# A gather ring of seven slots instead of eight, with one more output-projection slab kept for both tiles of a layer

## What is computed

```
for i in range(2):
    h = h + token_mixer(rms_norm(h), w_in[i], ..., w_o[i])     # proj = h @ w_in; attention; y @ w_o
    h = h + peer_ffn(rms_norm(h), w_query[i], sub_keys[i], u[i], v[i])
    h = h + sigmoid(rms_norm(h) @ w_ple_gate[i]) * (p[i] @ w_ple[i])
# peer_ffn, per token: 8 heads, 16 experts each, out of 128*128
ids, gate = top 16 of (top 16 of s1 + top 16 of s2), per head
pre = u[ids] . x;   out = sum over the 128 pairs of gate * gelu(pre) * v[ids]
```

## Time and profile before

| | us |
|---|---|
| median of three runs | 1560.29 |
| their range | 1559.32 to 1563.16 |
| the profiled execution, its own time | 1557.42 |
| its span, first to last instruction | 1555.6 |
| busy: PE / DVE / ACT / POOL | 1132.1 / 1069.5 / 567.9 / 575.4 |
| first gather issued at | 119.7 |
| last gather issued at | 1513.0 |

### The profile page before, as it was taken

How to read it: one execution, slowest core, us unless ns; L and a number is a source line. 1 busy time by engine, 2 the same in 40 slices (tenths; PEclk the granted TensorE clock), 3 DMA queues, 4 the chain that set the end, 5 groups by cost and what they waited for, 6 DMA issues and landing times.

```text
span 1555.6 us, 18293 instructions
## 1 busy us (share of the span) xinstructions
PE 1132.1 (73%) x6360; PEld 443.9 (29%) x6360; DVE 1069.5 (69%) x2719; ACT 567.9 (37%) x1788; POOL 575.4 (37%) x516
## 2 busy tenths in 40 slices
PE   9996676885658865778566887598555876676666
PEld 6771133351113422325111353245101311111112
DVE  3468986679987345567999536757799765454555
ACT  0503456333333235423333415733233443333332
POOL 0004444445443333435453323434444353333330
PEclk9996878997779978789668998989577976667668
DMA  9148999999999999999999999999999999999992
GB/s 358 65 173 362 416 421 400 403 421 421 421 421 395 418 417 417 422 418 404 421 421 417 417 418 420 403 391 414 420 421 421 399 423 421 421 421 422 422 420 112
DMA packets 90253, 607.35 MB, mean 390 GB/s; under 512 B 9904, under 2 KB 10416, under 8 KB 24624
## 3 DMA queue, kind: packets, MB, share of 16 engines
q0 software_dynamic: 73728, 536.90, 83.5%
q1 hardware_dynamic: 16272, 69.02, 11.2%
q10 hardware_dynamic: 160, 0.26, 0.1%
HBM read 605.09 MB, written 1.05 MB: 390 GB/s over the span
## 4 chain that ended last, share of the span: by engine, by line
DVE 34%; DMA 32%; PE 21%; ACT 6%; issue 4%; POOL 1%; ACTq 0%; POOLq 0%; DVEq 0%
DMA ring<-in_rows,ids 32%; DVE ring L1175 15%; PE acc L547 7%; PE bank L808 3%; PE bank L703 2%; DVE wb L1452 2%; POOL ring L514 1%; PE bank L876 1%; DVE y L1502 1%; PE bank L579 1%; DVE top_i L1459 1%; DVE top_i L1449 1%; PE bank L614 1%; PE bank L922 1%; ACT diag L964 1%
## 5 line engine op out<-in xcount | busy, mean ns | idle before, releaser
L514 POOL DMA_INDIRECT ring<-in_rows,ids x512 | 575.2, 1123 | 938.2 <-PE acc L547 760.9
L547 PE MATMUL acc<-ring,diag 64*64 64x512 f32 x3968 | 676.6, 791 | 328.6 <-ACT diag L964 326.0
L1175 DVE CUSTOM_DVE_ANT_0 ring<-ring,xc 128x1024 f32<-128x1024 f32 x504 | 605.9, 1223 | 356.1 <-DMA ring<-in_rows,ids 353.7
L955 ACT ACTIVATE gel<-pre 128x1 f32<-128x1 f32 x512 | 103.3, 202 | 805.9 <-DVE pre L1175 792.9
L547 PEld LDWEIGHTS acc<-ring,diag 64*64 64x64 f32 x3968 | 140.2, 161 | 813.7 <-ACT diag L964 703.6
L964 ACT ACTIVATE diag<-cst,act_w 128x64 f32<-128x64 f32 x512 | 178.1, 348 | 16.7
L961 ACT ACTIVATE act_w<-gate,gel 128x1 f32<-128x1 f32 x512 | 150.7, 294 | 16.6
L808 PE MATMUL bank<-hT,held 128*128 128x128 f32 x512 | 60.6, 278 | 2.5 <-DVE hT L1209 2.4
L808 PEld LDWEIGHTS bank<-hT,held 128*128 128x128 f32 x512 | 58.1, 192 | 12.5 <-issue 7.3
L703 PE MATMUL bank<-wring,hT 128*128 128x512 f32 x96 | 44.3, 604 | 5.6 <-DVE hT L1212 4.8
L1175 DVE DVE_READ_ACCUMULATOR2_ANT pre<- 128x1 f32 x512 | 42.1, 82 | 0.0
(11 more groups left out here) (272 smaller groups left out, 1075.8 us busy)
## 6 DMA issues: line engine op xcount, KB each, us to landing
wring<-in_w_in SPq DMA_DIRECT2D x16, 978.0 KB, 9.6
wring<-in_w_out SPq DMA_DIRECT2D x12, 1024.0 KB, 20.8
wring<-in_w_gate SPq DMA_DIRECT2D x11, 1024.0 KB, 14.0
held<-in_w_query SPq DMA_DIRECT2D x8, 1024.0 KB, 16.9
ring<-in_rows,ids POOLq DMA_INDIRECT x512, 13.9
ring<-in_w_in SPq DMA_DIRECT2D x8, 978.0 KB, 13.7
held<-in_w_out SPq DMA_DIRECT2D x2, 1024.0 KB, 11.2
held_latent<-in_w_latent SPq DMA_DIRECT2D x2, 768.0 KB, 16.2
```

The costliest lines, as they stand in the source:

```text
L514: pool.indirect_dma_start(out=ring[:, n % RING, :], out_offset=None, in_=rows, in_offset=bass.IndirectOffsetOnAxis(ap=index, axis=0),).the ...
L547: last = pe.matmul(acc[rows_of(c), r, :], diag[rows_of(r), j, :], ring[rows_of(r), j, D:][:, cols_of(c)], start=False, stop=True, skip_gro ...
L955: act.activation(gel[:, j:j + 1], pre[:, j:j + 1], ACT.Gelu).then_inc(gelued, 1)
L1175: dve.tensor_tensor_reduce(out=u, in0=u, in1=x, scale=1.0, scalar=0.0, op0=ALU.mult, op1=ALU.add, accum_out=pre[:, j:j + 1]).then_inc(dott ...
```

## The change

`RING` goes from 8 to 7: `ring` has seven slots, and with it `pre`, `gel`, `act_w`, `diag` and the seven semaphores of the rows. `HELD` goes from 5 to 6, so that two slabs of w_out (k = 2 and 3) are held per layer for both tiles, and only k = 0 and 1 go through `wring` for each tile. The eighth slab of w_in of layer 0 no longer has a ring slot; it is loaded into `lifts`. Since p is loaded into the same place, `load_p(0)` now waits until step 1 has used that slab (`slab_used` at 8), and it stands one place later in the SP program. In layer 1 the four query slabs and the keys are loaded in one place instead of two.

```
@@ -44,11 +44,11 @@
 PH, NKEY, TOPK = 8, 128, 16
 EXPERTS = NKEY * NKEY
 PAIRS = PH * TOPK
-RING = 8
+RING = 7
 WRING, WSLOT = 3, 2048
-HELD = KT // 2 + 1
+HELD = KT // 2 + 2
 KEPT = WRING
-OUT_HELD = KT // 2 - 1
+OUT_HELD = KT // 2 - 2
 NEG = -1e30
 TAIL = 8
 WHOLE = PAIRS - 2 * TAIL
@@ -270,6 +270,7 @@
         best_i = part_i[:, 1]
         pT = (lifts[:, 1, 0:2 * SEQ].rearrange("p (a s) -> p a s", a=2), kTf[:])
         hT_next = xc[:, 1, :].rearrange("p (k c) -> p k c", k=KT)
+        in_slab = [ring[:, k, 0:IN_W] for k in range(RING)] + [lifts[:].rearrange("p t c -> p (t c)")[:, 0:IN_W]]
         xc_tail = (xc[:, 0, :], lifts[:, 0, :])
         gain_tail = lifts[:, 1, 0:512]
         h_tail = wa[:, 0:1024].rearrange("p (r n) -> p r n", r=2)
@@ -427,7 +428,7 @@
             load(fb[:], forget_b.partition_broadcast(P), small_in)
             load(posi[:], pos, small_in)
             for k in range(KT):
-                load(ring[:, k, 0:IN_W], w_in[0, k * P:(k + 1) * P, :], slab_in[k])
+                load(in_slab[k], w_in[0, k * P:(k + 1) * P, :], slab_in[k])
                 if k == 1:
                     load(h[:, 1, :], x[P:2 * P, :], x_in[1])
             source = {
@@ -442,6 +443,10 @@
             def slab(i):
                 return held[:, i, :].rearrange("p (a n) -> p a n", a=2)
 
+            def load_out(l):
+                for k in range(OUT_HELD, KT // 2):
+                    load(slab(KT // 2 + k - OUT_HELD), source["out"](l, k), held_in[KT // 2 + k - OUT_HELD])
+
             def load_p(l):
                 load(pT[l], p_t[l * 2 * P:(l + 1) * 2 * P, :].rearrange("(a p) s -> p a s", p=P), pT_in[l])
 
@@ -451,23 +456,23 @@
                 l, t = layer_tile(s)
                 if n == 0:
                     load(held_latent[:], source["latent"](0, 0), held_latent_in)
+                if n == WRING - 1:
+                    load_out(0)
                 if n == WRING:
-                    load(slab(HELD - 1), source["out"](0, OUT_HELD), held_in[HELD - 1])
-                    for i in range(HELD - 1):
+                    for i in range(KT // 2):
                         load(slab(i), source["query"](0, i), held_in[i])
                     load(held_keys[:], source["keys"](0, 0), held_keys_in)
+                if n == WRING + 1:
+                    sp.wait_ge(slab_used, KT)
                     load_p(0)
                 if (kind, k, s) == ("in", 6, TILES):
                     sp.wait_ge(ids_ready, CHUNKS * TILES)
                     load(held_latent[:], source["latent"](1, 0), held_latent_in)
                 if (kind, k, s) == ("out", 0, TILES):
                     load(row_gain[:], ffn_g[1].partition_broadcast(P), row_gain_in)
-                    load(slab(HELD - 1), source["out"](1, OUT_HELD), held_in[HELD - 1])
+                    load_out(1)
                 if (kind, k, s) == ("out", 1, TILES):
-                    for i in range(2):
-                        load(slab(i), source["query"](1, i), held_in[i])
-                if (kind, k, s) == ("out", 2, TILES):
-                    for i in range(2, HELD - 1):
+                    for i in range(KT // 2):
                         load(slab(i), source["query"](1, i), held_in[i])
                     load(held_keys[:], source["keys"](1, 0), held_keys_in)
                 if (kind, k, s) == ("gate", 2, STEPS - 2):
@@ -629,7 +634,7 @@
                         next_of(hT_ready)
                     if s == 0:
                         pe.wait_ge(slab_in[k], 16)
-                        w = ring[:, k, :]
+                        w = in_slab[k]
                     else:
                         w = weights()
                     project(s, 0, k, w, hT)
@@ -654,13 +659,13 @@
                 if n == 10:
                     next_of(hT_ready, 2)
                 for k in range(*first):
-                    last = project(1, 0, k, ring[:, k, :], hT_next)
+                    last = project(1, 0, k, in_slab[k], hT_next)
                     if k == KT - 1:
                         last.then_inc(ahead_heads, 1)
                 if n == 35:
                     next_of(heads_ready, 6)
                 for k in range(*second):
-                    project(1, 1, k, ring[:, k, :], hT_next).then_inc(slab_used, 1)
+                    project(1, 1, k, in_slab[k], hT_next).then_inc(slab_used, 1)
 
             def leave(s, turn):
 
@@ -692,10 +697,10 @@
             def project_out(s, k):
 
                 l, t = layer_tile(s)
-                kept = k == OUT_HELD
+                kept = k >= OUT_HELD
                 if kept and t == 0:
-                    next_of(held_in[HELD - 1], 16)
-                w = held[:, HELD - 1, :] if kept else weights()
+                    next_of(held_in[KT // 2 + k - OUT_HELD], 16)
+                w = held[:, KT // 2 + k - OUT_HELD, :] if kept else weights()
                 g = min(k, 2)
                 first, stop = k <= 2, k != 2
                 for c in range(2):
@@ -703,7 +708,7 @@
                         last = pe.matmul(out_banks(s)[g][0][c][:, :], hT[:, 2 * k + a, :],
                                          w[:, a * D + c * 512:a * D + c * 512 + 512],
                                          start=(first and a == 0), stop=(stop and a == 1), skip_group_check=True)
-                    if kept:
+                    if k == KT // 2 - 1:
                         last.then_inc(out_half, 1)
                 if not kept:
                     release(last)
```

2 lines of the change are left out of this document (1 added, 1 removed).

## The result

The changed kernel takes **1583.33 us** (median of four runs, 1579.21 to 1586.66); the kernel before, run beside it, 1561.24 us. The ratio is 1.0144 with an interval of 1.0126 to 1.0162: 22 us slower. I had forecast slower, by 7.4 us, in a range from 1554.5 to 1578 us. The profiled execution of the change took 1586.66 us (span 1584.8 us), at the upper end of its runs, and that of before 1557.42 us, at the lower end of its own, so the two traces are 29 us apart and not 22.

The account below looks back on a forecast made before the run. The prediction took the DMA carrying the row stream from 120 to 1505 us as the bound. Its terms, -5.0 for two slabs and +12.4 for the slot, gave +7.4 us on 1560.29: 1567.7 us, range 1554.5 to 1578 us.

Parts of the forecast that it names:

- What bounds the kernel: From 120 to 1505 us, bytes moved by the DMA bound the kernel, plus 23 us in which the DMA is not full.
- Two slabs fewer: Two w_out loads of 1.049 MB go, for steps 1 and 3, inside the DMA-bound stretch: -5.0 us.
- One slot fewer: Seven ring slots: one row's carrying, 2.48 us, lost at each of five stops, +12.4 us; lower end zero, upper 19.8.
- The five charged stops: Near 272, 462, 845, 1010 and 1218 us, POOL waits 5.88 us or more for PE: 2.48 us each, 12.4 together.
- the dip at 1078 us: DMA rate falls to 392 GB/s there; it and other short dips were said to have short waits, costed at zero.
- the steady stretches: Last stage and choosing: one gather fewer leaves 5.2 and 4.3 under way, above the 3.9 enough at 1060 us; costed at nothing.
- The rule of the Trainium skill: A DMA takes about 2.0 us plus bytes at 436 GB/s; 4.4 us per gather, two under way nearly always enough, term near nothing.
- The loads at the start: Before the first gathers, w_in, w_out and p loads change place or wait; p has 8.8 us to land: nothing.
- Queries and keys in one place: Layer 1 loads: same bytes, landing before PE needs them, in a stretch where the DMA is full either way: nothing.
- The eighth first gather: At the stream's start it waits for row 0's use; seven earlier gathers need 17.4 us, row 0's matmul starts at 12.7: nothing.
- The ring's last slot is idle depth: Rival, 0.20: two or three gathers under way suffice and stops cost nothing, leaving -5.0 us, 1555.3 us.
- Dips deepen everywhere: Rival, 0.13: each of seven low-rate slices holds several stops, 23 us unfilled nearly doubles; +18 us, 1578 us and up.

Follow-up runs that it names:

- lim7_all: The kernel before with eight slots, POOL's wait one row stricter everywhere, so at most seven gathers are unfinished: 1.0171, 26.7 us slower.
- ladder: The kernel before with POOL's wait in the last stage allowing 6, 5, 4, then 3 unfinished gathers; run once for its trace, 1588.99 us.
- lifts8: The kernel before with eight slots, but the eighth w_in slab in the lifts table and p's load waiting for its use: 1.0021, 3.3 us slower.
- lim7_steady: The kernel before, at most seven unfinished gathers only in the first 34 rows, rows 89 to 127 of each window and the last stage from row 24: 1.0020, 3.1 us slower.
- ring7_only: The change without its w_out part (seven slots, eighth w_in slab in lifts, p waiting), against the kernel before: 1.0165, 25.8 us slower.

## Why the prediction was wrong

**Direction right, size wrong:** +7.4 us forecast, 22 us measured. By its own steps:

*What bounds the kernel* was right: the stream's rate sets the end, and nearly all that the change costs is unfilled DMA time (23 us by the windows before, 54 after).

*Two slabs fewer, -5.0 us:* right, -5.2 measured alone.

*One slot fewer, +12.4 us:* **this is the step that failed.** It measured 26.7 us in `lim7_all`. The five charged stops cost 12.5 us together. But I then wrote that the dip at 1078 us "and other short ones have short waits; I cost them at zero", and the rest of the dense stretches cost 15.1 us; and of the steady stretches "I cost them at nothing", which cost 3.1. The waits elsewhere were not short either. In the trace of before POOL waited eighteen times for PE as long as at the shortest stop that I charged or longer, the five included; one of the others, 10.39 us long, ends at 697.8 us. Two of the others, the second right ahead of the window that I took as proof of a full DMA:

```profile
164.03 0.94 POOL L514 DMA_INDIRECT ring<-in_rows,ids  x1 [7.59 <-PE acc L547]
...
1058.74 0.94 POOL L514 DMA_INDIRECT ring<-in_rows,ids  x1 [6.71 <-PE acc L547]
```
The 12.4 beside the 12.5 is luck in part. I had a stop cost a row only where the queue runs empty, "to zero", and nothing where a row's worth is left. In the trace of before 3, 1, 2, 1 and 3 gathers were still under way at the ends of the five waits; with one fewer, three of the five would by my own rule have cost nothing. They cost all the same, which fits the table above: the rate is down already at three and at two under way, there as in the stretches that cost 15.1 us.

The reason for both was one reading: 3.9 under way were enough at 1060 us, so I took the loss to begin only where the queue is empty. The ladder shows that 3.9 is the edge: 407 GB/s at 3.2 and 337 at 2.5. The kernel before spent 297 us at four under way, at 415 GB/s, and much of that time became three, at 399. The upper bound of this term, eight rows' carrying, 19.8 us, left out the same places, and so the range ended at 1578 us.

*The rule of the Trainium skill* that I set against my sum (DMA: Bandwidth & Descriptors, "Anatomy of one DMA — SWDGE (gpsimd) path") gives about 2.0 us plus the bytes at 436 GB/s, from which I had estimated 4.4 us for a lone gather, and two under way to fill the DMA. In the traces no gather lands in under 5.2 us. At 2.5 under way the measured rate is 337 of 422 GB/s, so by that estimate the slot would be nearly free, and by measurement it is not. My own division, 5.5 us of shortest landing over 2.48 us of carrying, gave 2.2, and was wrong in the same way: a gather that is issued into a busy DMA took 7.6 us with 2.5 under way, not 5.5.

*The loads at the start, "nothing":* too low. The w_out slab and p, 1.3 MB, went from a stretch with room to the front of the first gathers; the same with one more slab costs 3.3 us in `lifts8`. I had checked only whether p comes in time, not what its bytes displace. The changed kernel's own part of it is 0.7 us by the traces. p does come in time: PE's first products of p start at 127.71 us, and the wait before the first row's matmul is no longer than before.

```profile
127.71 4.13 PE L837 MATMUL bank<-wring,lifts 128*128 128x512 f32 x8
134.00 2.86 PE L552 MATMUL acc<-ring,diag 64*64 64x512 f32 x16 [2.16 <-ACT diag L969]
```
*Queries and keys in one place, "nothing":* nothing is seen of it; from row 136 to 176, where these loads are, the extra unfilled time grows by 0.2 us.

*The eighth first gather, "nothing":* up to row 24 the extra unfilled time is 1.8 us; these rows are among the steady ones of `lim7_steady`, whose whole cost is 3.1 us.

*The rivals.* "The ring's last slot is idle depth" is ruled out by `lim7_all`. "Dips deepen everywhere", 0.13, with its +18 us and up, is nearest to what happened: the unfilled time more than doubled, from 23 to 54 us, though not only in the seven low slices. I held against it that at 1060 us PE was busy throughout and the DMA full; one window says that this place is at the edge, not that others have room.

The parts add up within their intervals: 26.7 for the slot, less 5.2, plus 0.7 for the start is 22.2 us, and 22.5 were measured. That this is so close is luck. `ring7_only` has the start of `lifts8` in it, so by that pair the slot is 25.8 - 3.3 = 22.5 us and the sum 22.5 - 5.2 + 0.7 = 18.0 us. Each figure is uncertain by 1 to 3 us, and the slot is known only as 22 to 27 us.

Two slips of the prediction change nothing: its lower bound, 1560.29 - 5.0 - 1.0, is 1554.3 and not 1554.5 us, and its chances by its own split give slower 0.60 and same 0.30, not 0.58 and 0.32.

## What to carry to other kernels

Where a ring of buffers feeds a stream that the DMA bounds, count the time at each number of transfers under way and take the rate at one less for all of it (here that gave 38 us for 29 measured); the average sees none of the loss, and the places of the longest stops only half of it. Find the edge by making the wait stricter by one, which is a change of one number, before giving room away: here the ninth slot was worth 5 us, the eighth 22 to 27 and the seventh 58. And a load that waits for its place moves from a stretch with room into one without.

## What the runs showed of the hardware

Gathers of 1.05 MB (128 rows of 8 KB) needed four under way for the full 421 GB/s; with 3.2 it was 407, with 2.5 337, with 1.6 313 GB/s, and a gather still took 5.6 us from issue to landing with 1.6 under way. The rate at a given number from two up agreed within 6% between the five kernels of the table wherever that number stood for over 20 us.

Below four the 16 DMA engines are not simply idle. In the ladder's two lowest steps their busy share was still 0.92 and 0.91, against 1.01 at full rate, while the rate fell by 20% and 26%. The median packet of 8 KB took 309 ns there, as against 313 ns at full rate; but the slowest tenth took 436 ns and more with four allowed and about 600 ns and more with three, against 320 ns. So more than half of the loss is in a part of the packets that take longer, and the rest in engines without one. Why those packets are slow was not tried.
